# Expert gates streamed by fours of steps, and one one-hot token of eight made by GpSimd

## The reference

```python
def peer(h, w_pq, sub_keys, expert_u, expert_v):
    ...
    s_top, i_top = lax.top_k(scores, PEER_TOPK)
    cand = s_top[:, :, 0, :, None] + s_top[:, :, 1, None, :]
    cand_idx = i_top[:, :, 0, :, None] * N_KEYS + i_top[:, :, 1, None, :]
    best, pos = lax.top_k(cand.reshape(T, PEER_HEADS, -1), PEER_TOPK)
    idx = jnp.take_along_axis(cand_idx.reshape(T, PEER_HEADS, -1), pos, axis=-1)
    gate = jax.nn.softmax(best, axis=-1).astype(h.dtype)
    ...
        act = jax.nn.gelu(jnp.einsum('td,thkd->thk', tb, expert_u[ib]))
        return jnp.einsum('thk,thkd->td', gb * act, expert_v[ib])
```

## Time and profile before

| what | us |
|---|---|
| runs shown, median | 3693.1 |
| runs shown, lowest and highest | 3691.1, 3694.1 |
| profiled execution, its own time | 3696.8 |
| span of the profiled execution, first to last instruction | 3694.7 |
| busy in it: TensorE | 3577.7 |
| busy in it: VectorE | 2658.0 |
| busy in it: GpSimd | 1771.5 |
| busy in it: ScalarE | 547.8 |

### The profile page before, as it was taken

The page is one execution under the profiler, slowest core; times in us unless marked ns, Lnnn a source line. Parts: engine busy times, 40 slices in busy tenths (PEclk is TensorE's granted clock), DMA queues, the critical chain, the costliest instruction groups (busy, mean ns, idle before and its releaser), DMA issues. The chain is left out here.

```text
span 3694.7 us, 44814 instructions
## 1 busy us (share of the span) xinstructions
PE 3577.7 (97%) x15394; PEld 2493.7 (67%) x15394; DVE 2658.0 (72%) x5798; ACT 547.8 (15%) x1123; POOL 1771.5 (48%) x1531
## 2 busy tenths in 40 slices
PE   7999999999999999999989999989999999999998
PEld 3444578777777777766655456887777777776766
DVE  4523589897888777667765356998888787777777
ACT  3212215400000000000021121170000000000001
POOL 0011006666776566666501200357567766676663
PEclk8999999999999999999999999999999999999999
DMA  9711204999999999999951013099999999999997
GB/s 396 306 65 55 103 26 123 312 405 400 408 408 408 408 408 408 409 408 408 379 208 40 29 30 124 5 237 387 400 408 408 408 408 408 408 408 408 408 409 277
DMA packets 395015, 1114.45 MB, mean 302 GB/s; under 512 B 117264, under 2 KB 123536, under 8 KB 393600
## 3 DMA queue, kind: packets, MB, share of 16 engines
q0 software_dynamic: 175104, 637.61, 43.6%
q1 hardware_dynamic: 216416, 465.72, 34.2%
q10 hardware_dynamic: 3360, 9.57, 0.7%
HBM read 1067.63 MB, written 45.07 MB: 301 GB/s over the span
## 5 line engine op out<-in xcount | busy, mean ns | idle before, releaser
L1529 PE MATMUL ps<-big,y_nat 128*128 128x336 f32 x4096 | 1199.1, 446 | 2.3 <-ACT big L1623 2.3
L1529 PEld LDWEIGHTS ps<-big,y_nat 128*128 128x128 f32 x4096 | 774.3, 190 | 334.6 <-ACT big L1623 2.7
L1933 DVE SCALAR_TENSOR_TENSOR big<-big,kn_area 128x1024 f32<-128x1024 f32 x608 | 782.8, 1288 | 165.9 <-DMA big<-in_peer_v,gates_area 160.1
L1915 DVE CUSTOM_DVE_ANT_0 big<-big,y_nat 128x1024 f32<-128x1024 f32 x608 | 740.3, 1224 | 127.3 <-DMA big<-in_peer_u,gates_area 124.2
L2130 POOL DMA_INDIRECT big<-in_peer_u,gates_area x512 | 656.3, 1282 | 349.0 <-DVE kn_area L1915 223.7
L2141 POOL DMA_INDIRECT big<-in_peer_v,gates_area x512 | 579.2, 1131 | 352.7 <-DVE big L1933 238.9
L1542 PEld LDWEIGHTS ps<-gates_area,y_nat 128*128 128x128 f32 x2048 | 366.9, 191 | 63.0 <-issue 62.9
L1542 PEld LDWEIGHTS ps<-gates_area,big 128*128 128x128 f32 x2048 | 363.7, 190 | 61.2 <-issue 61.2
L1649 ACT ACTIVATE gates_area<-ps 128x336 f32<-128x336 f32 x256 | 114.9, 449 | 1885.9 <-PE ps L1529 1877.3
L1542 PE MATMUL ps<-gates_area,y_nat 128*128 128x208 f32 x2048 | 383.9, 341 | 0.0
L1542 PE MATMUL ps<-gates_area,big 128*128 128x208 f32 x2048 | 381.0, 339 | 0.0
(11 more groups left out here) (300 smaller groups left out, 3325.5 us busy)
## 6 DMA issues: line engine op xcount, KB each, us to landing
y_nat<-in_peer_ut SPq DMA_DIRECT2D x256, 512.0 KB, 6.8
y_nat<-in_peer_v SPq DMA_DIRECT2D x128, 512.0 KB
big<-in_peer_v SPq DMA_DIRECT2D x128, 512.0 KB, 7.7
big<-in_w_mod SPq DMA_DIRECT2D x24, 2048.0 KB, 13.6
expert_gates<-big SPq DMA_DIRECT2D x10, 3584.0 KB, 16.0
big<-expert_gates SPq DMA_DIRECT2D x64, 280.0 KB, 7.5
gates_area<-expert_gates SPq DMA_DIRECT2D x64, 280.0 KB, 6.8
big<-in_w_in SPq DMA_DIRECT2D x8, 2048.0 KB, 15.8
```

Of the source, the lines that this page charges most:

```text
L1529: last = pe.matmul(ps[:, 6 + par, 0:NX], u_s[par][:, k, :], h_t[:, k, X0:ND], start=(k == 0), stop=(k == KD - 1))
L1915: dve.tensor_tensor_reduce(out=u_ring[at], in0=u_ring[at], in1=y_nat[:, tile, :], scale=1.0, scalar=0.0, op0=ALU.mult, op1=ALU.add, accum_ ...
L1933: dve.scalar_tensor_tensor(out=acc, in0=v_ring[:, k % VSLOTS, :], scalar=wact[:, k:k + 1], in1=acc, op0=ALU.mult, op1=ALU.add).then_inc(s_ ...
```

## The change

Two things are changed in each layer.

First, gates are stored and loaded for four expert blocks at a time (QUAD = 4). gate_dram has 32 entries of 128 x 1120 instead of 64 of 128 x 560; a store has rows of 896 B, a load (gate_quad) is 560 KB in rows of 4480 B. SyncE issues one load in every four steps, behind the scores stream and ahead of the values stream of the fourth. Its loop is unrolled to eight steps, so that the place of a load is fixed. The larger place 0 begins at big[20480] and reaches beyond 21504, where hot1 begins; so load 0 is issued only once TensorE has done all groups (a wait for s_f), behind load 1, and the first block of v goes after it. Places of other buffers are moved to make room.

Second, of the eight tokens of a group, the first one-hot of one (WHOLE = 1) is no longer compared by VectorE nor scaled by the wide multiply: GpSimd makes it from iota_k in one instruction (compare with the key, multiply by the weight, both read from choice_t). VectorE's first comparison has 7 x 128 elements, the second still 8 x 128. GpSimd's new instruction waits for the free buffer (s_f) and stands ahead of its multiply, which now has 4 or 5 x 128 elements; s_oh2 counts two per group.

```diff
+QUAD = 4
...
+WHOLE = 1
...
-        gate_dram = nc.dram_tensor("expert_gates", (N_KEYS // 2, P, 2 * GW), F32, kind="Internal").ap()
+        gate_dram = nc.dram_tensor("expert_gates", (N_KEYS // QUAD, P, QUAD * GW), F32, kind="Internal").ap()
...
-        g_s = [big[:, 20480:20480 + 2 * GW], gates_area[:, 2560 + 4 * NX:2560 + 4 * NX + 2 * GW]]
+        g_s = [big[:, 20480:20480 + QUAD * GW], gates_area[:, 2560 + 3 * NX:2560 + 3 * NX + QUAD * GW]]
...
                         sp.wait_ge(s_fe, BY_BLOCK * (b + 1))
-                        sp.dma_start(gate_dram[:, :, 2 * KEPT * b:2 * KEPT * (b + 1)].rearrange("q p t -> p q t"),
-                                     gate_s[b % 2].rearrange("p (q s) t -> p q (s t)", s=2)).then_inc(s_gst[b % 2], 16)
+                        sp.dma_start(gate_dram[:, :, QUAD * KEPT * b:QUAD * KEPT * (b + 1)].rearrange("q p t -> p q t"),
+                                     gate_s[b % 2].rearrange("p (q s) t -> p q (s t)", s=QUAD)).then_inc(s_gst[b % 2], 16)
...
-                    gate_pair(sp, 0, 0)
-                    gate_pair(sp, 1, 1)
+                    gate_quad(sp, 1, 1)
                     sp.wait_ge(s_sbe, 2 * PH + 1)
+                    sp.wait_ge(s_f, GROUPS)
+                    gate_quad(sp, 0, 0)
                     v0()
+
                     def gates_of(q, place):
 
-                        sp.wait_ge(s_h, 2 * q - 2)
-                        gate_pair(sp, q, place)
-
-                    scores_of(2, 0, 1)
-                    with sp.Fori(0, N_KEYS // 4 - 1) as m:
+                        sp.wait_ge(s_h, QUAD * q - QUAD)
+                        gate_quad(sp, q, place)
+
+                    def four_steps(m, gates=None):
+
                         for n in range(4):
                             scores_of(3 + 4 * m + n, 1 - n % 2, 2 + 4 * m + n)
-                            if n % 2 == 0:
-                                gates_of(2 + 2 * m + n // 2, n // 2)
+                            if n == 3 and gates is not None:
+                                gates_of(m + 2, gates)
                             values_of(2 + 4 * m + n, n % 2, 1 + 4 * m + n)
+
+                    scores_of(2, 0, 1)
+                    with sp.Fori(0, N_KEYS // 8 - 1) as m:
+                        four_steps(2 * m, 0)
+                        four_steps(2 * m + 1, 1)
+                    four_steps(N_KEYS // 4 - 2)
...
-                        pe.wait_ge(s_oh2, n + 1)
+                        pe.wait_ge(s_oh2, (WHOLE + 1) * (n + 1))
...
-                        wide = [P, OCT, N_KEYS]
-                        for q, hot in enumerate((hot1, hot2)):
-                            dve.tensor_tensor(hot[:, n % HOTS, :, :], iota_k[:, :].unsqueeze(1).broadcast_to(wide),
-                                              ps[:, 4 + i % 2, q * P + OCT * g:q * P + OCT * (g + 1)].unsqueeze(2).broadcast_to(wide),
+                        for q, hot, m in ((0, hot1, OCT - WHOLE), (1, hot2, OCT)):
+                            dve.tensor_tensor(hot[:, n % HOTS, 0:m, :], iota_k[:, :].unsqueeze(1).broadcast_to([P, m, N_KEYS]),
+                                              ps[:, 4 + i % 2, q * P + OCT * g:q * P + OCT * g + m].unsqueeze(2).broadcast_to([P, m, N_KEYS]),
                                               ALU.is_equal).then_inc(s_oh, 1)
...
-                        rest = hot1[:, n % HOTS, some:OCT, :]
+                        if n >= HOTS:
+                            pool.wait_ge(s_f, n + 1 - HOTS)
+                        for tt in range(OCT - WHOLE, OCT):
+                            t = OCT * g + tt
+                            pool.tensor_scalar(hot1[:, n % HOTS, tt, :], iota_k[:, :], choice_t[:, i % 2, t:t + 1],
+                                               choice_t[:, i % 2, 2 * P + t:2 * P + t + 1], ALU.is_equal, ALU.mult).then_inc(s_oh2, 1)
+                        rest = hot1[:, n % HOTS, some:OCT - WHOLE, :]
                         pool.wait_ge(s_oh, 2 * n + 1)
-                        pool.tensor_tensor(rest, rest, choice_t[:, i % 2, 2 * P + OCT * g + some:2 * P + OCT * (g + 1)].unsqueeze(2)
-                                           .broadcast_to([P, OCT - some, N_KEYS]), ALU.mult).then_inc(s_oh2, 1)
+                        pool.tensor_tensor(rest, rest, choice_t[:, i % 2, 2 * P + OCT * g + some:2 * P + OCT * (g + 1) - WHOLE].unsqueeze(2)
+                                           .broadcast_to([P, OCT - WHOLE - some, N_KEYS]), ALU.mult).then_inc(s_oh2, 1)
```

More of the change, by code:

```diff
@@ L139, in build @@
         big = sb("big", [P, 32000])
-        gates_area = sb("gates_area", [P, 4480])
+        gates_area = sb("gates_area", [P, 4688])
         kn_area = sb("kn_area", [P, 2560])
@@ L262, in build @@
         u_ring = [big[:, 5120 + n * D:5120 + (n + 1) * D] for n in range(USLOTS - 1)] + [big[:, 19456:20480]]
-        v_ring = carve(big, 21504, VSLOTS, D)
-        acc = big[:, 29696:30720]
+        v_ring = carve(big, 21600, VSLOTS, D)
+        acc = big[:, 29792:30816]
         s_cin = sem("condition_loaded")
-        v_s = [big[:, 30720:31744], y_nat[:, 2, :]]
+        v_s = [big[:, 30816:31840], y_nat[:, 2, :]]
         u_s = [y_nat[:, n, :].rearrange("p (k e) -> p k e", e=P) for n in range(2)]
-        gelu_s = [gates_area[:, 2560 + n * NX:2560 + (n + 1) * NX] for n in range(2)]
-        h_s = [gates_area[:, 2560 + n * NX:2560 + (n + 1) * NX] for n in (2, 3)]
-        g_s = [big[:, 20480:20480 + 2 * GW], gates_area[:, 2560 + 4 * NX:2560 + 4 * NX + 2 * GW]]
[L271 to L274, removed]
+        gelu_s = [gates_area[:, 2560:2560 + NX], kn_area[:, 2048:2048 + NX]]
+        h_s = [gates_area[:, 2560 + n * NX:2560 + (n + 1) * NX] for n in (1, 2)]
+        g_s = [big[:, 20480:20480 + QUAD * GW], gates_area[:, 2560 + 3 * NX:2560 + 3 * NX + QUAD * GW]]
+        part_idx = carve(kn_area, 2464, 1, P // PARTS, dt=U32)
+        part_gate = carve(kn_area, 2464 + P // PARTS, 1, P // PARTS)
+        a_idx = kn_area[:, 2464 + 2 * P // PARTS:2464 + 2 * P // PARTS + XA].bitcast(U32)
+        a_gate = kn_area[:, 2464 + 2 * P // PARTS + XA:2464 + 2 * P // PARTS + 2 * XA]
         y_turned = carve(big, 5120, KD, 2 * P)
@@ L1334, in build, with gate_quad @@
             by_ranks = lambda v: v.rearrange("p (a b) -> p a b", b=TOPK)
-            def gate_pair(sp, q, place):
+            def gate_quad(sp, q, place):
                 sp.dma_start(g_s[place], gate_dram[bass.ds(q, 1)].rearrange("a p t -> p (a t)")).then_inc(s_gs[place], 16)
@@ L1897, in weigh @@
                         dve.wait_ge(s_ge, j + 1)
-                        dve.wait_ge(s_gs[j // 2 % 2], 16 * (j // 4 + 1))
+                        dve.wait_ge(s_gs[j // QUAD % 2], 16 * (j // (2 * QUAD) + 1))
                         if past is not None:
@@ L1901, in weigh @@
                         dve.tensor_tensor(by_block(h_s[par]), by_block(gelu_s[par]),
-                                          g_s[j // 2 % 2].rearrange("p (b s t) -> p b s t", s=2, t=KEPT)[:, :, par, :], ALU.mult)
+                                          g_s[j // QUAD % 2].rearrange("p (b s t) -> p b s t", s=QUAD, t=KEPT)[:, :, j % QUAD, :], ALU.mult)
                         dve.tensor_tensor(h_s[par][:, GW:NX], gelu_s[par][:, GW:NX], gate_s[1][:, j, :], ALU.mult).then_inc(s_h, 1)
```

## The result

The changed kernel takes 3636.1 us (median; 3635.4 to 3637.8) against 3693.1 us: ratio 0.9845, 95% interval 0.9832 to 0.9857. The prediction had 3677.3 us and a range that ended at 3667. The direction was right and the size was not: 57 us gained, not 15.8. The profiled execution has a span of 3633.3 us.

The account below looks back on a forecast made before the run. VectorE was taken to bound the gates stage, TensorE the dense stage until step 18, DMA engines its end. Terms 5.6 + 0.2 + 2.1 = 7.9 us per layer, 15.8 in all, took 3693.1 to 3677.3 us; range 3667 to 3692.

Parts of the forecast that it names:

- in the dense stage still the gathered rows, 27 us of which only 2 go: End of each dense stage: late gathered rows cost 27 us, and the change was to remove only 2 of them.
- Part 1: Gates stage: VectorE compares 7 + 8 tokens instead of 8 + 8, 0.134 us less per group, 5.6 us per layer.
- Part 2: Gates stage: GpSimd's new compare-and-scale of 128 elements takes 0.5 us and hides behind VectorE.
- Rival A: Gates stage: GpSimd becomes the bound, from 0.98 us per new instruction; at 1.4 us, 3712 us in all; chance 0.08.
- Part 3: Gates stage: stores in rows of 896 B land in about 13 us instead of 16, hidden, no cost and no gain.
- My bound of 1 us a layer: End of the gates stage: if stores got no faster, ScalarE and the stage's end would be some 1 us late per layer.
- Part 4: Dense stage from step 18 on: gate loads by four steps halve their packets, 2.1 us per layer, bounds 0 and 2.5.
- The fixed 10 ns per packet: Transfers: each packet costs a fixed 10 ns plus some 36.6 ns per 1000 B, taken from two weight streams.
- The late first load: Start of the dense stage: the first load of four waits for TensorE's last group, issued 1.3 us earlier than before, costing nothing.
- Part 5: Start of the dense stage: GpSimd's gathers start earlier, worth almost nothing; bounds 0 to 3 us per layer, taken as 0.
- The deeper hole before step 18: Dense stage before step 18: transfers already run dry there, and an earlier start of the gathers makes that hole larger.
- the last sign of being wrong: Dense stage: the prediction fails if its length changes by more than 5 us, which nothing in it prices.

## Why the prediction was wrong, step by step

**The sum has no term for the moved buffers.** Places were taken as free, and never named as a part. The rows held a constant that I used as a property of the transfers, 408 GB/s, when it was one of this kernel's places. The step that failed is the one that follows from it: "in the dense stage still the gathered rows, 27 us of which only 2 go". All of them went (23, as 4 of the 27 were TensorE's own). In the earlier trace rows's stretch of 400 us the rows of v are 106 of about 314 equal portions of 512 KB (213 gathered rows, 88 streamed blocks, 22 gate loads of 0.55 portions), 34%, and alone they brought 408 to 416 GB/s. That is 2% for all from a third of the transfers. The streamed block, 22 portions of 314 or 7%, brought 408 to 410, 0.5%. Shared out over the transfers moved, either makes some 6 or 7% each, but the packet times above say that this is the wrong way to share it out: everything moved by 128 B brings only 3% (408 to 419 GB/s), and the first third brings most of that, because other packets get shorter with it. Why they do, no run shows.
At the start of the kernel, where all transfers were moved by 128 B, a packet of 4096 B takes 159.5 ns for 164.0, 3% less. With three buffers moved by 64 B its time (163.4 ns) and the rate (408 GB/s) are those of the old places. With the moved gates_area, where g_s[1] lies 1344 B further down, the packets of 2240 B fell from 95.7 to 94.2 ns on the mean of both places. That the places decide is shown, for the moves tried; by which mechanism is open.

**Part 1, comparisons: right.** 0.133 us for 0.134. Groups now come 2.13 us apart (two in 4.26 us in the second layer), 2.136 predicted. The stage is 5.0 us shorter for 5.8 with its end: in the first groups VectorE has to wait for TensorE to free a buffer, and that wait grew from 2.5 us to 3.3.

**Part 2, GpSimd: right in the verdict, wrong in the size.** 795 ns, the value that I set aside as an upper end (774 ns), for 500. It hides, but barely. In the timeline of the gates stage the second group of a pair follows without idle:

```profile
2424.47 0.80 POOL L2126 TENSOR_SCALAR big<-iota_k,gates_area 128x128 f32<-128x128 f32 x1
...
2425.35 1.04 POOL L2130 TENSOR_TENSOR big<-big,gates_area 128x512 f32<-128x512 f32 x1
...
2426.38 0.80 POOL L2126 TENSOR_SCALAR big<-iota_k,gates_area 128x128 f32<-128x128 f32 x1
...
2427.48 1.26 POOL L2130 TENSOR_TENSOR big<-big,gates_area 128x640 f32<-128x640 f32 x1 [0.30 <-DVE big L1899]
```

1.26 + 0.80 + 1.04 + 0.80 = 3.90 us of every 4.26. Rival A began at 0.98 us; 0.18 us more per instruction would have brought it about. By the same sum a second token for GpSimd would not fit.

**Part 3, stores: right in time (13 us), wrong in value.** "No cost, no gain" held only for this part by itself. With the one-hots and the old stores the gates stages are 0.4 us longer than with the new ones, and the dense stages, which transfers bound there, 1.0 to 1.4 us longer than before: some 3 us in all, as far as single profiles tell. My bound of 1 us a layer was near, but I had not followed the late store into the gathers. The price of a packet held: 43 ns for 896 B predicted, 43.3 in the trace.

**Part 4, loads: about right, as far as it shows.** I had 2.1 us a layer, 2.5 at most. In the run of the changed kernel with v's buffers 128 B further the dense stages are 1177.3 and 1178.4 us; with the same places of gates_area and the old loads they are 1182.4 and 1182.6. That is 5.1 and 4.2 us, but the stretches behind them grew by 2.6 and 2.8 us (521.4 to 524.0 and 13.6 to 16.4), so that 2.5 and 1.4 us are left. The medians say the same: 3687.5 - 3673.3 = 14.2 us, less 10.5 for the one-hots, 3.7 for two layers where the sum had 4.2. Once TensorE sets the pace it is 0.7 us in all. The fixed 10 ns per packet came from two streams that were both at the old places; with all buffers moved by 128 B packets of 2240 B take 91.0 ns (kernel before) and packets of 4480 B 173.0 (changed kernel), which is 9 ns fixed. How much of the gain is packets and how much the earlier start of the gathers, no run separates.
The late first load did no harm, as said: issued at 2456.65, the first weighting at 2464.45, the products at 2466.89, 9.15 us behind the first scores as before. One reading was wrong, though: not "the same 0.57 MB of gates" stood in line but twice that, as load 1, also 560 KB, was issued 0.9 us ahead of load 0. In the second layer the first weighting starts when the load lands, without slack.

**Part 5, the early start.** GpSimd still waits 2.2 us for the last store. The deeper hole before step 18 that I named is there (2560 to 2680 us, 3 us per value, steps 11 to 24):

```profile
GB/s 419 419 418 422 421 419 412 418 347 332 360 369 365 345 395 411 424 402 421 385 401 414 273 363 406 411 421 411 415 418 410 418 418 425 422 416 418 418 421 419
```

**The sum against its own ground.** With v's buffers 128 B further the change gives 19.5 us, but 5.6 of them go with gates_area's places, by their own run. That leaves 13.9 us for the parts that the sum had at 15.8. So the terms were about right, within what the runs can tell; the missing one, the places, is worth 44.0 us in the kernel before by itself, 37 us of it in the changed kernel from v's buffers. The rivals were all about the parts that I had listed, so none could hold it, and the lower end of the range was set by the largest of them. Only the last sign of being wrong caught it: "if the dense stage changes by more than 5 us, which nothing here prices".

## What to carry to other kernels

When a change moves buffers, the moves are a part of it with a price, whatever they were made for: where transfers are the bound, run the kernel before with the moves and nothing else. Here moves by 384 B took 41 us off, and those by 64, 512 and 1024 B nothing that the runs can tell. When a rate stands at the same value in every slice, ask what holds it there before it is used as a constant; here one unused tensor of 128 B moved it, and took 46 us off. Test a large surprise by halves of the diff, the parts "of no effect" first.

## What the runs showed of the hardware that I had not expected

A move of buffers by 128 B changed the speed of transfers: 159.5 against 164.0 ns a packet of 4096 B, 414 against 405 GB/s, at the start of the kernel with all of them 128 B further; in the dense stage v's ring alone, a third of the transfers, moved by 384 B took the rate from 408 to 416 GB/s and made packets shorter that were not moved (163.4 to 160.3 ns). Three buffers moved by 64, 512 and 1024 B stayed at 408 GB/s. GpSimd's compare-and-scale of 128 elements with two scalars per partition takes 795 ns, while 128 elements more in its plain multiply add only 213 ns; how much of the 795 is fixed and how much is the form, no run separates. Stores of 3.67 MB in rows of 896 B ran at 342 to 378 GB/s and landed in 13.1 us; in rows of 448 B they mostly ran at 223 to 344 GB/s and landed in 16.0.
